# The level products of a gated recurrence as elementwise products summed by a matrix of ones, with level and output work ahead of the weight split and matmul chunks in pairs

## The chip, the cores and the metric

The kernel runs on one core of a Trainium2 chip. The metric is the time of the whole kernel on the device in microseconds (us). The engines of the core that work here are TensorE (PE in the profile, its weight loads PEld), VectorE (DVE), ScalarE (ACT), a little GpSimd (POOL) at the start, and SyncE (SP), whose queue issues the weight loads from HBM.

## What is computed

A trunk of two layers over 256 tokens of width 2048. Layer 0 mixes tokens by a gated linear recurrence (HGRN2), layer 1 by a short gated convolution; each is followed by a gated feed-forward part with 5632 hidden features. Only the recurrence matters here:

```python
D_MODEL = 2048; SEQ = 256; HGRN_HEADS = 16; HGRN_EXPAND = 128; CHUNK = 64

def chunked_gated_recurrence(q, k, v, logf):
    """S_t = diag(f_t) S_{t-1} + k_t v_t^T, o_t = S_t^T q_t, in chunkwise form."""
    ...

def hgrn2_mixer(xn, w_in, lb, out_gain, w_out):
    proj = xn @ w_in
    q, fr, v, g = jnp.split(proj, [HGRN_F_DIM, 2 * HGRN_F_DIM, 2 * HGRN_F_DIM + HGRN_I_DIM], axis=-1)
    q = jax.nn.silu(q.astype(jnp.float32)) * (HGRN_EXPAND ** -0.5)
    f = lb + (1.0 - lb) * jax.nn.sigmoid(fr.astype(jnp.float32))
    k = 1.0 - f
    logf = jnp.log(f)
    o = chunked_gated_recurrence(heads(q), heads(k), heads(v), heads(logf))
    o = rms_norm(o, out_gain) * jax.nn.silu(g.astype(jnp.float32))
    return (o @ w_out.astype(jnp.float32)).astype(xn.dtype)
```

So the output of token t of a head is the sum over s up to t of A[s, t] v_s, where A[s, t] is the dot product, over the head's 128 features, of q_t, k_s and the product of the gates f between s and t.

## The kernel before

**Weights.** Every projection is cut into chunks of 512 input by 256 output features. A chunk is loaded by SP into one of four buffers of `raw`, then split into two parts so that the product keeps float32 accuracy: ACT copies it with rounding to `w_parts[..., 0, :]` (high part, `split` of the scalar block, L325), and DVE subtracts that from the raw value into `w_parts[..., 1, :]` (low part, L542). In the feature-major form PE runs eight 512-column matmuls of the high part (`feature_highs`, L1041) and then eight 256-column matmuls of the low part (`feature_lows`, L1051). In the value group (`V_GROUP`, group 2) the output is token-major: `token_boths` (L1064, both weight parts as the moving operand, counts `lo_used`), then `token_highs` (L1073, counts `hi_used`). ACT may overwrite the buffer of chunk c for chunk c+4 when `hi_used` has counted chunk c; DVE waits for `lo_used` and for ACT's `hi_ready`.

**Phases.** `HGRN_IN` has 4 iterations of 4 groups (gate f, query q, value v, output gate) of 8 chunks each; an iteration serves 4 heads. `HGRN_OUT` has 2 iterations of 2 groups of 8. Then come the two feed-forward parts and the convolution mixer. The steps of a group are in `Phase.steps`; the engines walk the same steps, each with its own program, and meet by semaphores only. PE works a chunk at a time in `HGRN_IN`, `HGRN_OUT` and `DOWN1`, and elsewhere in runs of `RUN` = 2: highs of both chunks, then lows of both.

**Levels.** A is built by nested halves (`LEVELS` = 1, 2, 4 ... 128): the level with half length n pairs a token in the second half of a block of 2n with one in the first. For each level DVE makes `ql` and `kl` (`level_operands`, L769 to L786), PE multiplies them per head as plain float32 128x128 matmuls into the PSUM buffer `side` (L1204), and DVE merges the result into `a_diag` by a mask (`take_stage`, L815). The diagonal is level -1: eight such matmuls of `qh` and `kh` (L1199). DVE carries the prefix products of gates along in `fpre` and `suf` (`prefixes`). `PLAN` says after which chunk of the pair of groups 2 and 3 PE issues which level; numbers above 15 lie in the next iteration. The last stage is the output (`output`, L1183), twelve matmuls of `a_diag`, `a_off` and `vt`.

**Order on DVE and ACT.** At each chunk position DVE first runs the split of the chunk four ahead, then sums a finished accumulator with ACT's copy (`corrected`), then the rest (`pieces`): merge of a level, prefixes, operands. The output is copied from PSUM to `o_sb`, multiplied by gain and gate, split into `act` (`output_steps`, L838 to L849); ACT squares `o_sb`. `act` of iteration 3 is what the last chunks of the first `HGRN_OUT` group wait for.

## Time and profile before

| | |
|---|---|
| time, median of 3 runs | 2345.23 us (2345.22 to 2345.57) |
| the profiled execution | 2345.17 us, span 2343.4 us |
| PE busy | 2330.2 us, 99% |
| DVE busy | 1698.6 us, 72% |
| ACT busy | 1045.2 us, 45% |
| iteration 2 of HGRN_IN (154.04 to 255.94) | 101.90 us, DVE busy 83.64 us |
| HBM | 185 GB/s over the span |

The span is the profiler's, from the first to the last instruction; 1.8 us lie around it. A busy PE is not a PE at its peak, since its matmuls overlap, so the cadence (start to start) tells more than the busy share. The four iterations of HGRN_IN end at about 415 us, HGRN_OUT at about 509 us.

### The profile page before, as it was taken

How to read it: one execution, taken by the hardware profiler on the slowest of the kernel's cores; microseconds unless marked ns; L12 is line 12 of the kernel's file. 1: busy time of each engine (PE TensorE's matmuls, PEld its weight loads, DVE VectorE, ACT ScalarE, POOL GpSimd, SP SyncE). 2: the span in 40 equal slices, each digit the busy share in tenths (PEclk: the TensorE clock that was granted, in tenths of full speed). 3: DMA queues.
4: the chain of work that ended last, by engine and by line, in shares of the span. 5: the costliest groups of instructions: out<-in, count | busy, mean ns of one | idle time of the engine just before them, and what ended most of it. 6: DMA issues, size and time to landing. Idle time of an engine off the chain costs nothing.

```text
span 2343.4 us, 37300 instructions
## 1 busy us (share of the span) xinstructions
PE 2330.2 (99%) x13212; PEld 2048.8 (87%) x13212; DVE 1698.6 (72%) x2151; ACT 1045.2 (45%) x1146; POOL 2.7 (0%) x8
## 2 busy tenths in 40 slices
PE   9999999999999999999999999999999999999998
PEld 8888888888888888888888888888888888888887
DVE  8879788778788788865455766666788788785444
ACT  7344443454444444444444444444444444443443
POOL 0000000000000000000000000000000000000000
PEclk9999999999999999999999999999999999999999
DMA  7555555556656566665656665565656656665564
GB/s 254 159 172 153 166 171 155 179 181 189 188 179 197 186 188 189 188 193 187 194 184 190 186 192 187 186 193 178 198 183 193 192 179 192 190 206 187 191 191 158
DMA packets 410284, 434.93 MB, mean 186 GB/s; under 512 B 13264, under 2 KB 386384, under 8 KB 410064
## 3 DMA queue, kind: packets, MB, share of 16 engines
q1 hardware_dynamic: 409616, 431.53, 59.1%
q10 hardware_dynamic: 576, 2.16, 0.3%
q8 instruction: 59, 0.97, 0.2%
q14 instruction: 33, 0.27, 0.0%
HBM read 431.54 MB, written 2.10 MB: 185 GB/s over the span
## 4 chain that ended last, share of the span: by engine, by line
PE 96%; DVE 2%; DMA 1%; issue 1%; ACT 0%; SPq 0%; DVEq 0%; ACTq 0%
PE acc L1041 54%; PE acc L1051 28%; PE acc L1088 3%; PE acc L1086 3%; PE acc L1087 3%; PE acc L1064 2%; PE side L1204 1%; PE acc L1073 1%; PE side L1183 0%; DMA h<-in_x 0%; DVE w_parts L542 0%; DMA raw<-in_hgrn_w_in 0%; PE side L1199 0%; ACT w_parts L325 0%; DVE kl L778 0%
## 5 line engine op out<-in xcount | busy, mean ns | idle before, releaser
L542 DVE TENSOR_TENSOR w_parts<-raw,w_parts 128x1024 fp32r<-128x1024 f32 x816 | 982.2, 1222 | 575.1 <-PE acc L1051 348.3
L325 ACT ACTIVATE w_parts<-raw 128x1024 fp32r<-128x1024 f32 x816 | 858.1, 1058 | 1023.0 <-PE acc L1041 801.8
L1041 PE MATMUL acc<-xn,w_parts 128*128 128x512 f32 x4352 | 1049.4, 391 | 1.5 <-ACT w_parts L325 1.3
L1041 PEld LDWEIGHTS acc<-xn,w_parts 128*128 128x128 f32 x4352 | 796.5, 188 | 154.0 <-issue 1.5
L1051 PEld LDWEIGHTS acc<-xn,w_parts 128*128 128x128 f32 x4352 | 564.2, 191 | 25.1
L1051 PE MATMUL acc<-xn,w_parts 128*128 128x256 f32 x4352 | 572.4, 283 | 0.0
L1041 PE MATMUL acc<-act,w_parts 128*128 128x512 f32 x1216 | 293.6, 391 | 0.7 <-DVE act L849 0.7
L1041 PEld LDWEIGHTS acc<-act,w_parts 128*128 128x128 f32 x1216 | 222.5, 188 | 43.3 <-DVE act L849 0.9
L1051 PEld LDWEIGHTS acc<-act,w_parts 128*128 128x128 f32 x1216 | 158.0, 191 | 7.2
L1051 PE MATMUL acc<-act,w_parts 128*128 128x256 f32 x1216 | 160.2, 283 | 0.0
L1086 PE MATMUL acc<-w_parts,act 128*128 128x512 f32 x352 | 137.3, 390 | 0.0
L1088 PE MATMUL acc<-w_parts,act 128*128 128x512 f32 x352 | 137.0, 389 | 0.0
L1087 PE MATMUL acc<-w_parts,act 128*128 128x512 f32 x352 | 137.0, 389 | 0.0
L339 ACT ACTIVATE corr<-acc 128x512 f32<-128x512 f32 x144 | 85.7, 595 | 76.0 <-PE acc L1051 76.0
L624 DVE SCALAR_TENSOR_TENSOR tb<-pad,par,tb 128x256 f32<-128x256 f32 x208 | 90.9, 481 | 12.2 <-DVE tb L622 0.3
L624 DVE SCALAR_TENSOR_TENSOR ta<-pad,par,ta 128x256 f32<-128x256 f32 x176 | 77.5, 481 | 11.9
L1088 PEld LDWEIGHTS acc<-w_parts,act 128*128 128x128 f32 x352 | 66.1, 188 | 13.8
L1087 PEld LDWEIGHTS acc<-w_parts,act 128*128 128x128 f32 x352 | 66.1, 188 | 13.6
L1086 PEld LDWEIGHTS acc<-w_parts,act 128*128 128x128 f32 x352 | 66.1, 188 | 13.4
L575 DVE TENSOR_TENSOR pad<-acc,corr 128x512 f32<-128x512 f32 x96 | 65.5, 682 | 0.0
L369 ACT ACTIVATE xn<-h,par 128x256 fp32r<-128x256 f32 x64 | 28.6, 500 | 76.8 <-DVE h L662 59.8
L401 ACT ACTIVATE ta<-ta 128x1024 f32<-128x1024 f32 x22 | 23.4, 1063 | 82.6 <-DVE ta L624 82.6
(125 smaller groups left out, 1024.7 us busy)
## 6 DMA issues: line engine op xcount, KB each, us to landing
raw<-in_ffn_w_up SPq DMA_DIRECT2D x352, 512.0 KB, 3.7
raw<-in_ffn_w_down SPq DMA_DIRECT2D x176, 512.0 KB, 4.5
raw<-in_hgrn_w_in SPq DMA_DIRECT2D x128, 512.0 KB, 3.7
raw<-in_sc_w_in SPq DMA_DIRECT2D x96, 512.0 KB, 4.5
raw<-in_hgrn_w_out SPq DMA_DIRECT2D x32, 512.0 KB, 3.6
raw<-in_sc_w_out SPq DMA_DIRECT2D x32, 512.0 KB, 4.4
h<-in_x SPq DMA_DIRECT2D x4, 512.0 KB, 7.3
final_w<-in_final_norm ACTq DMA_DIRECT2D x1, 1024.0 KB, 7.3
```

The lines of the kernel that those rows point to most:

```text
L325: nc.scalar.activation(w_parts[:, c % RING, :, 0, :], raw[:, c % RING], ACT.Copy).then_inc(hi_ready, 1)
L339: o = nc.scalar.activation(corr[:], acc[:, a % SETS, :, T:], ACT.Copy)
L369: o = nc.scalar.activation(xn[:, bass.ds(tile + j, 1), 0, :], h[:, bass.ds(tile + j, 1), :], ACT.Copy, scale=par[:, bass.ds(weight + tile ...
L542: v.tensor_tensor(w_parts[:, c % RING, :, 1, :], raw[:, c % RING], w_parts[:, c % RING, :, 0, :].bitcast(F32), ALU.subtract).then_inc(lo_r ...
L575: o = v.tensor_tensor(dst[:, part * TW:(part + 1) * TW, :], acc[:, a % SETS, :, 0:T], corr[:], ALU.add)
L624: o = v.scalar_tensor_tensor(out=dst[:, j, :], in0=src, scalar=w, in1=dst[:, j, :], op0=ALU.mult, op1=ALU.add)
L1041: o = mm(to[:, j, :], w[:, q, 0, j * P:(j + 1) * P], src[:, k * KW + q, :, :].rearrange("p n t -> p (n t)"), start=begin and q == 0, stop= ...
L1051: o = mm(to[:, j, T:], w[:, q, 1, j * P:(j + 1) * P], src[:, k * KW + q, 0, :], start=False, stop=end and q == KW - 1, skip_group_check=True)
L1064: o = mm(to[:, b, :], x_block(src, k * KW + q, 0, b), w[:, q].rearrange("p n d -> p (n d)"), start=begin and q == 0, stop=False, skip_grou ...
L1086: mm(bank, x_hi, hi, start=begin and q == 0, stop=False)
L1087: low = mm(bank, x_hi, lo, start=False, stop=False)
L1088: high = mm(bank, x_lo, hi, start=False, stop=end and q == KC - 1)
```

## The change

Four things change.

1. The diagonal and the first level are no longer matmuls of queries with keys. DVE multiplies elementwise (`qh * kh` into `tb`; `ql * kh` into `kl[:, 0]`), ACT rounds the product to its high part (`product_high_parts`), DVE makes the low part (`product_low_parts`), and PE sums over the 128 features by a matrix of ones in float32r matmuls of 512 columns: four for the diagonal, two for the first level. Every row of the result is the same, and the mask picks the place. The parts of the diagonal lie in `act`'s last tiles (`own_parts`).
2. PE works in pairs of chunks in HGRN_IN (but for its very first group) and HGRN_OUT (but for two chunks of its first group). A stage due after an even chunk number then stands between the highs and the lows of a pair.
3. On DVE the level work (merge, prefixes, operands) and the output work stand ahead of the split of the same position, with explicit waits for `stage_done`. `PLAN` puts the diagonal after chunk 3 instead of 2, levels 0 to 3 one chunk later too, and the output after position 17 instead of 18.
4. The output is read straight from PSUM by DVE and ACT (`o_sb` is gone). The first group of HGRN_OUT takes its chunks in another order, in which the part that needs `act` of iteration 3 is at place 6 instead of 5.

```diff
+        elif first and g == 0 and self is HGRN_OUT:
+            order = [(0, 0), (0, 1), (1, 0), (1, 1), (0, 2), (1, 2), (0, 3), (1, 3)]
...
+    def runs(self, first, g, end):
+        single = self is DOWN1 or self is HGRN_IN and first and g == 0
+        paired = 0 if single else self.cpg - RUN if self is HGRN_OUT and first and g == 0 else end
+        return [range(k, k + RUN) for k in range(0, paired, RUN)] + [range(k, k + 1) for k in range(paired, end)]
...
-PLAN = [(2, LEVEL, -1), (3, LEVEL, 0), (5, LEVEL, 1), (6, LEVEL, 2), (8, LEVEL, 3), (10, LEVEL, 4),
-        (12, LEVEL, 5), (13, LEVEL, 6), (15, LEVEL, 7), (18, OUTPUT, 0)]
+PLAN = [(3, LEVEL, -1), (4, LEVEL, 0), (6, LEVEL, 1), (7, LEVEL, 2), (9, LEVEL, 3), (10, LEVEL, 4),
+        (12, LEVEL, 5), (13, LEVEL, 6), (15, LEVEL, 7), (17, OUTPUT, 0)]
...
+            def product_high_parts(i, g, kk):
+                if (g, kk) in ((2, 1), (2, 2)):
+                    act_e.wait_ge(product_ready, at(i, 2, kk))
+                    nc.scalar.activation(own_parts[:, 0] if kk == 1 else pair_parts[:, 0],
+                                         tb[:].rearrange("p j t -> p (j t)") if kk == 1 else
+                                         kl[:, 0].rearrange("p j t -> p (j t)"), ACT.Copy).then_inc(product_hi_ready, 1)
-            phase_of(HGRN_IN, hgrn)
+            phase_of(HGRN_IN, hgrn, ahead=product_high_parts)
...
+                if n == 1:
+                    link(v.tensor_tensor(q_to, halves(qh[:], n)[:, :, 1], pre[:, :, 1], ALU.mult), i)
+                    v.tensor_tensor(kl[:, buf].rearrange("p j (w n) -> p (j w) n", n=n), q_to, halves(kh[:], n)[:, :, 0],
+                                    ALU.mult).then_inc(product_ready, 1)
...
+            def product_low_parts(i, n, product, parts):
+                dve.wait_ge(product_hi_ready, at(i, 2, n + 1))
+                v.tensor_tensor(parts[:, 1], product.rearrange("p j t -> p (j t)"), parts[:, 0].bitcast(F32),
+                                ALU.subtract).then_inc(product_parts_ready, 1)
...
-                    v.tensor_scalar(kl[:, 1], mirrored(fpre[:, :, P:]), -1.0, 1.0, ALU.mult, ALU.add)
...
+                    v.tensor_tensor(tb[:], qh[:], kh[:], ALU.mult).then_inc(product_ready, 1)
+                if n == 1:
+                    product_low_parts(i, 0, tb[:], own_parts)
+                if n == 2:
+                    product_low_parts(i, 1, kl[:, 0], pair_parts)
+
+            def levels(i, first, g, kk):
+                last_take(i, g, kk)
+                if not first:
+                    output_steps(i - 1, g, kk)
+                n = g * HGRN_IN.cpg + kk - 2 * HGRN_IN.cpg
+                done = [stage for stage, (after, what, _) in enumerate(PLAN) if what == LEVEL and n == after + 1]
+                for stage in done:
+                    dve.wait_ge(stage_done, at(i, HGRN_STAGES, S_HGRN + stage + 1))
+                    v.sem_inc(stage_seen, 1)
+                for after, what, m in PLAN:
+                    if what == LEVEL and 0 <= m < len(LEVELS) - 1 and n == operands_at(after, m) + 1:
+                        prefixes(i, m)
                 for after, what, m in PLAN:
-                    if what == LEVEL and m >= 0 and n == after - LEAD:
+                    if what == LEVEL and m >= 0 and n == operands_at(after, m):
                         level_operands(i, m)
+                for stage in done:
+                    take_stage(i, stage)
...
-                        run = 1 if phase in (HGRN_IN, HGRN_OUT, DOWN1) else RUN
-                        for k0 in range(0, phase.cpg - RING * ends_here, run):
+                        for run in phase.runs(first, g, phase.cpg - RING * ends_here):
...
+                        if m < 1:
+                            parts, halves = (own_parts, 2) if m < 0 else (pair_parts, 1)
+                            pe.wait_ge(product_parts_ready, at(i, 2, m + 2))
+                            steps = [lambda to, c=c, n=n: mm(to[:, c * GC:(c + 1) * GC], sum_ones[:],
+                                                             parts[:, n, c * GC:(c + 1) * GC], start=(n == 0),
+                                                             stop=(n == 1))
+                                     for c in range(halves) for n in range(2)]
```

On DVE, at the first two positions of the value group of an iteration of HGRN_IN, before (`w_parts` is a weight split, `qh` the query, `ql` and `kl` the operands of the first level):

```order
L542 TENSOR_TENSOR w_parts<-raw,w_parts 128x4x256 [waits lo_used,hi_ready]
L904 SCALAR_TENSOR_TENSOR qh<-ta,tb 128x1024 [waits gate_sig]
L542 TENSOR_TENSOR w_parts<-raw,w_parts 128x4x256 [waits lo_used,hi_ready]
L769 TENSOR_TENSOR ql<-qh,fpre 128x512 [waits chain]
L776 COPY kl<-kh 128x256 x2
L781 MEMSET suf 128x512
L782 COPY suf<-fpre 128x512
```

and of the change:

```order
L569 TENSOR_TENSOR w_parts<-raw,w_parts 128x4x256 [waits lo_used,hi_ready]
L937 SCALAR_TENSOR_TENSOR qh<-ta,tb 128x1024 [waits gate_sig]
L940 TENSOR_TENSOR tb<-qh,kh 128x1024 [waits qk_ready]
L797 TENSOR_TENSOR ql<-qh,fpre 128x512 [waits chain]
L798 TENSOR_TENSOR kl<-ql,kh 128x512 [waits chain]
L800 MEMSET suf 128x512
L801 COPY suf<-fpre 128x512
L569 TENSOR_TENSOR w_parts<-raw,w_parts 128x4x256 [waits lo_used,hi_ready]
L818 TENSOR_TENSOR act<-tb,act 128x1024 [waits product_hi_ready]
```

The product `tb` and the level's operands now stand ahead of the second split, and the low part of the product (L818) behind it.

On ACT, at the same two positions and the one behind them, of the change (`act` is the high part of the diagonal's product, `pair_parts` that of the first level's; before, the splits stood there with the sigmoid of `tb` alone between the first two):

```order
L340 ACTIVATE w_parts<-raw 128x4x256 [waits hi_used]
L462 ACTIVATE tb<-ta 128x1024 [waits scaled_ready]
L470 ACTIVATE act<-tb 128x1024 [waits product_ready]
L340 ACTIVATE w_parts<-raw 128x4x256 [waits hi_used]
L470 ACTIVATE pair_parts<-kl 128x512 [waits product_ready]
L340 ACTIVATE w_parts<-raw 128x4x256 [waits hi_used]
```

The high part of the product stands ahead of the second split, and waits for DVE's product.

On PE, in the first group of HGRN_OUT from its first chunk that needs `act` of iteration 3 on, before:

```order
L1041 MATMUL acc<-act,w_parts 128x512 [waits hi_ready,act_ready]
L1041 MATMUL acc<-act,w_parts 128x512 x7
L1051 MATMUL acc<-act,w_parts 128x256 [waits lo_ready]
L1051 MATMUL acc<-act,w_parts 128x256 x7
L1041 MATMUL acc<-act,w_parts 128x512 [waits hi_ready]
L1041 MATMUL acc<-act,w_parts 128x512 x7
```

and in the change, from the pair ahead of it:

```order
L1101 MATMUL acc<-act,w_parts 128x512 [waits hi_ready]
L1101 MATMUL acc<-act,w_parts 128x512 x7
L1111 MATMUL acc<-act,w_parts 128x256 [waits lo_ready]
L1111 MATMUL acc<-act,w_parts 128x256 x7
L1111 MATMUL acc<-act,w_parts 128x256 [waits lo_ready]
L1111 MATMUL acc<-act,w_parts 128x256 x7
L1101 MATMUL acc<-act,w_parts 128x512 [waits hi_ready,act_ready]
L1101 MATMUL acc<-act,w_parts 128x512 x7
```

The last wait for `act_ready` has moved from the sixth chunk of the group to the seventh, behind three pairs.

## Rows read from the trace of the kernel before

**Rows 1.** The page: the span, and each engine's busy time, share and instructions.

```profile
span 2343.4 us, 37300 instructions
PE 2330.2 (99%) x13212; PEld 2048.8 (87%) x13212; DVE 1698.6 (72%) x2151; ACT 1045.2 (45%) x1146; POOL 2.7 (0%) x8
```

**Rows 2.** PE's waits: engine, line, releaser, us in total, times, longest us.

```profile
PE side L1204 <- DVE kl L778: 2.3, 4, 0.6
PE acc L1041 <- DVE act L849: 0.7, 1, 0.7
```

**Rows 3.** The chain in a phase of pairs: start us, us, what.

```profile
537.85 3.65 PE acc L1041 x16
...
632.49 3.65 PE acc L1041 x16
```

**Rows 4.** PE's timeline in HGRN_OUT: start, us, engine, line, out<-in, xcount.

```profile
441.95 2.00 PE L1041 MATMUL acc<-act,w_parts 128*128 128x512 f32 x8
...
481.06 1.32 PE L1041 MATMUL acc<-act,w_parts 128*128 128x512 f32 x5
```

**Rows 5.** PE's timeline around the last level of iteration 2.

```profile
210.45 1.06 PE L1204 MATMUL side<-ql,kl 128*128 128x128 f32 x8
211.26 2.09 PE L1041 MATMUL acc<-xn,w_parts 128*128 128x512 f32 x8
213.19 1.11 PE L1051 MATMUL acc<-xn,w_parts 128*128 128x256 f32 x8
214.14 2.00 PE L1041 MATMUL acc<-xn,w_parts 128*128 128x512 f32 x8
215.98 1.12 PE L1051 MATMUL acc<-xn,w_parts 128*128 128x256 f32 x8
```

**Rows 6.** PE's timeline: the diagonal's first matmul, and the first behind it.

```profile
165.21 0.39 PE L1199 MATMUL side<-qh,kh 128*128 128x128 f32 x2
...
166.91 0.47 PE L1064 MATMUL acc<-w_parts,xn 128*128 128x512 f32 x1
```

**Rows 7.** The third level's stage in iteration 2: DVE's operands, then PE.

```profile
179.83 0.75 DVE L778 TENSOR_TENSOR kl<-kh,suf 128x256 f32<-128x256 f32 x2
...
179.86 0.28 PE L1073 MATMUL acc<-w_parts,x_mirror 128*128 128x256 f32 x1
180.71 0.48 PE L1204 MATMUL side<-ql,kl 128*128 128x128 f32 x2 [0.58 <-DVE kl L778]
```

**Rows 8.** PE's timeline: the wait for `act` in HGRN_OUT.

```profile
430.84 1.11 PE L1051 MATMUL acc<-act,w_parts 128*128 128x256 f32 x8
432.61 2.11 PE L1041 MATMUL acc<-act,w_parts 128*128 128x512 f32 x8 [0.65 <-DVE act L849]
```

**Rows 9.** The value group's start in iteration 2: PE, ACT and DVE.

```profile
156.83 0.40 PE L1064 MATMUL acc<-w_parts,xn 128*128 128x512 f32 x1
...
159.82 1.06 ACT L325 ACTIVATE w_parts<-raw 128x1024 fp32r<-128x1024 f32 x1 [2.11 <-PE acc L1073]
160.79 1.04 ACT L443 ACTIVATE tb<-ta 128x1024 f32<-128x1024 f32 x1
...
160.92 1.23 DVE L542 TENSOR_TENSOR w_parts<-raw,w_parts 128x1024 fp32r<-128x1024 f32 x1 [0.66 <-ACT w_parts L325]
162.06 1.22 DVE L904 SCALAR_TENSOR_TENSOR qh<-ta,tb 128x1024 f32<-128x1024 f32 x1
```

**Rows 10.** DVE's timeline: split of position 3, and the last level's key operand.

```profile
171.09 1.23 DVE L542 TENSOR_TENSOR w_parts<-raw,w_parts 128x1024 fp32r<-128x1024 f32 x1 [2.60 <-ACT w_parts L325]
...
208.13 0.67 DVE L771 TENSOR_TENSOR kl<-kh,suf 128x512 f32<-128x512 f32 x1
```

**Rows 11.** PE's opening matmuls (L1169) in two stretches: busy us (count), clock, DMA.

```profile
1.00:4.60 3.60, 3.52 (x16) 3.55 (x17) 1.00 0.73 226
4.60:6.60 2.00, 2.00 (x18) 1.86 (x16) 1.00 1.06 400
```

More of the change, by code:

```diff
@@ L212, in trunk @@
         stage_free = sem("stage_free")
+        stage_seen = sem("stage_seen")
         inits = sem("inits")
@@ L340, in correction, with phase_of @@
                 o.then_inc(corr_ready, 1)
-            def phase_of(phase, pieces, peel_last=False):
+            def phase_of(phase, pieces, peel_last=False, ahead=None):
                 def body(i, first):
@@ L420, in output_steps @@
                 if (g, kk) == (0, 3):
[L421 to L422 removed]
+                    s = S_HGRN + HGRN_STAGES - 1
+                    act_e.wait_ge(act_ready, at(i, 1, 1))
+                    nc.scalar.activation(qh[:], side[:, s % STAGES].rearrange("p (j t) -> p j t", j=TG), ACT.Square) \
+                        .then_inc(sq_ready, 1)
             def hgrn(i, first, g, kk):
@@ L519, in body @@
                             if ahead:
-                                ahead(i, g, kk)
+                                ahead(i, first, g, kk)
                             early = first and phase is HGRN_IN and g == 0
@@ L634, in normed, with residual_phase @@
                 add_squares(i, 4, sq + part, sq + part, ta[:, part * TW:(part + 1) * TW, :])
-            def residual_phase(phase, r0, sq0, weight, rs_n=None, rs_stage=None):
+            def residual_phase(phase, r0, sq0, weight, rs_n=None, rs_stage=None, ahead=None):
                 carry = carried.pop() if carried else None
@@ L665, in pieces @@
                         normed(i, phase, r, sq, part, tile, weight)
-                phase_of(phase, pieces, into=lambda g: tb)
+                phase_of(phase, pieces, ahead=ahead, into=lambda g: tb)
             def up_phase(phase, n, rs_n, rs_stage, conv):
@@ L877, in hgrn @@
                     rms(0, S_RS_HGRN, T + 2)
-                for stage, (after, _, _) in enumerate(PLAN):
-                    if n == after + 1:
-                        take_stage(i, stage)
                 if kk == last and g != V_GROUP:
@@ L894, in hgrn @@
                     v.tensor_scalar(kh[:], fpre[:], -1.0, 1.0, ALU.mult, ALU.add)
-                    v.tensor_scalar(kl[:, 1], mirrored(fpre[:, :, P:]), -1.0, 1.0, ALU.mult, ALU.add)
-                for after, what, m in PLAN:
-                    if what == LEVEL and 0 <= m < len(LEVELS) - 1 and n == after - LEAD + 1:
-                        prefixes(i, m)
                 if not first:
-                    output_steps(i - 1, g, kk)
+                    output_sums(i - 1, g, kk)
                 if n == 0:
@@ L905, in hgrn, with last_output @@
                                            op0=ALU.mult, op1=ALU.mult).then_inc(qk_ready, 1)
-                    dve.wait_ge(qk_ready, at(i, 1 + len(LEVELS), 1))
+                    dve.wait_ge(qk_ready, at(i, len(LEVELS), 1))
+                    v.tensor_tensor(tb[:], qh[:], kh[:], ALU.mult).then_inc(product_ready, 1)
[11 more added lines that the diff above has]
+                    dve.wait_ge(stage_done, at(i, HGRN_STAGES, S_HGRN + stage + 1))
+                    v.sem_inc(stage_seen, 1)
                 for after, what, m in PLAN:
-                    if what == LEVEL and m >= 0 and n == after - LEAD:
+                    if what == LEVEL and 0 <= m < len(LEVELS) - 1 and n == operands_at(after, m) + 1:
+                        prefixes(i, m)
+                for after, what, m in PLAN:
+                    if what == LEVEL and m >= 0 and n == operands_at(after, m):
                         level_operands(i, m)
-            phase_of(HGRN_IN, hgrn, ahead=last_take, into=lambda g: ta)
+                for stage in done:
+                    take_stage(i, stage)
+            phase_of(HGRN_IN, hgrn, ahead=levels, into=lambda g: ta)
             late[0] += 4 * HGRN_IN.n
-            carried.append(lambda g, kk: output_steps(HGRN_IN.n - 1, g, kk))
-            residual_phase(HGRN_OUT, 0, 8, NORM_FFN, 1, S_RS_OUT)
+            carried.append(lambda g, kk: output_sums(HGRN_IN.n - 1, g, kk))
+            def last_output(i, first, g, kk):
+                if first:
+                    output_steps(HGRN_IN.n - 1, g, kk)
+            residual_phase(HGRN_OUT, 0, 8, NORM_FFN, 1, S_RS_OUT, ahead=last_output)
             up_phase(UP0, 0, 2, S_RS_UP0, FFN_CONV)
@@ L1149, in body @@
                             if phase is DOWN1:
-                                between(i, first, g, k0)
+                                between(i, first, g, run[0])
                                 continue
-                            for kk in range(k0, k0 + run - 1):
+                            for kk in run[:-1]:
                                 between(i, first, g, kk)
@@ L1159, in body @@
                                     feature_lows(to, c, src, k, end)
-                            between(i, first, g, k0 + run - 1)
+                            between(i, first, g, run[-1])
                         if ends_here:
```

95 lines of the change are left out of this document (47 added, 48 removed).

## The prediction

> **What bounds the kernel now.** The page's busy shares come first: PE is busy 99% of the span, DVE 72%, ACT 45% [rows 1]. So the time is PE's, and an edit is worth what it takes from PE's own stream or from its waits. PE's waits come next, and they are few: four on a level's operands, 2.3 us, and one on the activations of HGRN_OUT, 0.7 us [rows 2]. The rest is cadence. I therefore read PE's timeline by starts, and then the timelines of DVE and ACT where the change puts new work between them and PE. An iteration of HGRN_IN takes 101.9 us; whatever is found in it counts four times.
>
> **The change part by part.**
>
> *Pairs.* In the phase of pairs 17 pairs lie between the two starts shown, 94.64 / 17 = 5.567 us each [rows 3]. Chunk by chunk 14 chunks take 39.11 us, 2.794 each, 5.587 per two [rows 4]. A pair saves 0.020 us. HGRN_IN gets 60 pairs (4 iterations of 16, less 4 in its first group), HGRN_OUT 15: 75 x 0.020 = **-1.5 us**. That a stage falls inside a pair changes the count of switches between highs and lows by none.
>
> *A level's stage now.* Four float32 matmuls take 0.81 us to the next start, and the eight matmuls behind them need 1.93 where an undisturbed eight need 1.84: 0.90 us in all [rows 5]. The diagonal has eight of them: 166.91 - 165.21 = 1.70, plus the same 0.09, 1.79 us [rows 6].
>
> *The stages as sums by ones.* The trace has no matmul with a matrix of ones in this format, but it has 512-column matmuls of the same format by the thousand: 3.65 / 16 = 0.228 us [rows 3]. Four are 0.91 us, two 0.46. They can't be quicker, since they stream the same columns; if they paid the 0.09 us of a change of operand [rows 5], they would be 1.00 and 0.55. I take the lower, because they are of the format of their neighbours. Diagonal 1.79 - 0.91 = 0.88, first level 0.90 - 0.46 = 0.44; 1.32 x 4 = **-5.3 us** (-4.6 at the other end).
>
> *Waits that go.* Before the third level PE pauses: 180.71 - 179.86 = 0.85 where 0.12 is the cadence, 0.73 us, and some 0.1 us of restart behind it, as the stage behind a pause is that much longer in the timeline. The change gives that level one more chunk. 0.84 x 4 = **-3.4 us** [rows 2, 7]. In HGRN_OUT PE starts at 432.61 where 430.84 + 0.95 = 431.79 was due, a wait of 0.82 [rows 8]. Now the output comes one chunk earlier and the chunk that needs it one later, and DVE does its product ahead of the split: 5.6 us more room. **-0.8 us**. What is late next there is the root of the norm; its start moves by 0.6 us (one accumulator is summed ahead of it), and PE asks for the next splits more than a microsecond after they are ready.
>
> Without anything new, these make -11.0 us. Now what is new.
>
> *The wait that comes: the product's way to PE.* The diagonal's product goes DVE, ACT, DVE, and weight splits stand in between on both. I time it from the start of the value group (156.83 in iteration 2 [rows 9]), with the durations of rows 9: an ACT pass over 1024 elements 1.06, 0.97 to the next start; a DVE pass 1.22 or 1.23, 1.14 to the next start; 0.04 from ACT's end to DVE's start (160.88 to 160.92), which I take for DVE's own result and for DVE to ACT too.
>
> - ACT may split chunk 4 when `hi_used` has counted chunk 0. Now this is at 2.79, and ACT starts at 2.99 [rows 9]. In pairs the eight highs of chunk 1 come in front: 3.65 + 0.95 = 4.61, ACT at 4.81.
> - DVE's split 1.10 later, as in rows 9: 5.91. The query at 7.05, done 8.27. The product at 8.31, done 9.53.
> - ACT's next instruction is the product's high part, 9.57. Only then its split of chunk 5, 10.55 to 11.61.
> - DVE has meanwhile made the first level's operands (0.67 us and less each [rows 10]; done about 11.5). It waits for that split: 11.65. Its low part of the product starts at 12.79, done 14.01.
> - PE gets it 0.13 us later, as with the level before (180.58 to 180.71 [rows 7]): **14.14**.
>
> PE gets there after two pairs: 2 x 5.567 = **11.13**. So it waits 3.0 us, plus the 0.1 of restart: 3.1 us, in each iteration, **+12.4 us**. Queued behind it is all of PE's work. Who waits in turn is nobody in need: chunk 4 and 5 are split by 7.1 and 12.9, and due at 15.1 and 16.9. The uncertainty is the hand-over times, eight of them, and whether the splits between are of the usual length: 2.6 to 3.6 us, 10.4 to 14.4 in all.
>
> *DVE behind that wait.* DVE gains three passes over the products and a product more (about 3.5 us) and loses the copy of the output and the small key copies (about 2.3). In the trace it works from the split of position 3 (171.09) to the last level's key operand (208.80) with hardly a pause, 37.7 us [rows 10]. In the change that split starts at 12.79 + 1.14 + 1.14 + two passes over 512 elements (0.67 or less) = 16.3 to 16.4; one split fewer (1.14) lies on the way, as levels now stand ahead of it: ready at 16.4 + 37.7 - 1.1 = 53.0. PE comes to the last level at 14.14 + 0.1 + 0.91 + 12 chunks (33.4) + 0.46 + six levels (5.4) = 54.4. So DVE arrives 1.4 us early, and for the level before, by the same count, about 1. The wait at the diagonal pays for this: without it PE would be there at 51.3, and DVE late by 1.8. DVE's six new marks (`stage_seen`) have no row of their own; between nothing and the 0.13 us hand-over of rows 7 each, 0 to 0.8 us. I take it that they fit.
>
> *Others at nothing.* The ones' memset is behind POOL's own first ones. Reading the output in PSUM costs DVE as much as reading the copy; ACT's square starts after the product. The output one position earlier: `a_off` is merged ahead of the split at the iteration's end and PE needs it two chunks later. SP's loads wait for the low splits; the latest of these is the one at 12.9, and its load is needed nine us later.
>
> **Sum.** -1.5 - 5.3 - 3.4 - 0.8 + 12.4 = +1.4 us. The profiled execution took 2345.17 us against a median of 2345.23, so they can stand for each other: **2346.6 us**. The gain in PE's stream is real and a new wait eats it. A measurement of this kernel can tell about 0.2%, 4.7 us, from no change.
>
> **The rivals.**
>
> *The wait does not come, or is short.* If ACT or DVE were through by 11.13, all of the first part would count, less what DVE owes at the last level: -11.0 + 4 x 1.8 = -3.8 at the worst, -11.0 at best, **2334 to 2341**, 2337 in the middle. For it: in the trace the query is made as late as 162.06 only because ACT's split is, and a smaller hand-over or another order in the queues would move all. Against it: the seven steps are all in program order with a semaphore each, and three microseconds are two and a half DVE passes. 11%.
>
> *TensorE's clock falls in the pause* (the slower side). The opening matmuls show both levels: 16 records in 3.6 us, then 18 in 2.0 [rows 11], so 1.2 GHz and then 2.4 GHz, though the clock column reads 1.00 in both. PE's pauses in the trace are all much shorter than 3 us, and none is followed by slow matmuls. If this one were, the work behind it would run at half rate as long as the opening did, 3.6 us, and lose 1.8 us: 2346.6 + 4 x 1.8 = **2353.8**. It decides from the pause that is long enough for the clock to fall, which no row shows; the stream before and behind is dense. 7%.
>
> The Trainium skill ("TensorE: Matmul & The Clock Gate", the section on HAM oscillation) says that a kernel whose matmul bursts are parted by pauses can be throttled again at each pause and start every burst cold. That is this rival; the trace has no pause to test it on.
>
> *DVE becomes the bound behind the wait.* Once the marks and waits cost DVE over 1 us more than counted by position 11 to 13, PE waits at the last two levels. Each further microsecond is 4 us in all; at 1.0 over, **2350.6**. For it: DVE has no pause in that stretch. Against: the count keeps one merge in reserve. 14%.
>
> *The stages save nothing* (operand changes cost what the columns save): +5.3, 2351.9; it needs the sums by ones to be twice as slow as every row of their kind. 2%.
>
> **How the numbers follow.** The forecast has 66%, with its own range 2344 to 2349.5 from the wait's 10.4 to 14.4 us and the stage's 0.7. The range of eight in ten takes in the upper part of the first rival and the DVE case: 2340 to 2351. Faster by over 0.2% (under 2340.5): 11% of the first rival, less its slow end, and a little of the forecast: 0.12. Slower by over 0.2% (over 2349.9): the clock, half of the DVE case, the stages and the forecast's edge: 0.16. Within: 0.72.
>
> **What would show it.** PE's waits after: a releaser DVE, the subtraction into `act`, four times about 3 us, and no wait on `kl` nor on HGRN_OUT's activations. The stage of the diagonal 0.9 us, that of the first level 0.46. An iteration of 102.4 us instead of 101.9. DVE without a pause from the second split of the value group to the last level. If the matmuls behind the pause have a cadence of 0.43 us, the clock fell. I am wrong if ACT's high part of the product starts well before 9.6 us from the group's start, or if the last levels show waits.

## The result and the profile after

| | before | changed |
|---|---|---|
| median of 11 executions | 2345.23 us | 2351.47 us |
| lowest and highest | 2344.91, 2345.60 | 2346.86, 2354.06 |
| profiled execution, its span | 2345.17, 2343.4 | 2348.86, 2347.0 |
| ratio, 95% interval | | 1.0023 (1.0015 to 1.0031) |

The change makes the kernel 0.15 to 0.31% slower. The forecast was 2346.6 us, the range 2340 to 2351. The median of all executions lies 0.5 us above the range; the ratio times 2345.23 gives 2350.6, just inside. The kernel before had 0.7 us between its lowest and highest execution. Now it is 7.2 us, and that spread is the first thing to explain: the lowest execution is the forecast to 0.3 us.

The page of the changed kernel, first the span and busy times, as in [rows 1]:

```profile
span 2347.0 us, 37183 instructions
...
PE 2325.6 (99%) x13140; PEld 2044.5 (87%) x13140; DVE 1703.4 (73%) x2151; ACT 1050.2 (45%) x1154; POOL 2.8 (0%) x9
```

PE has 4.6 us less to do and a span 3.6 us longer. Its waits, answering to [rows 2]:

```profile
PE side L1259 <- DVE act L818: 11.1, 4, 2.8
PE acc L1101 <- ACT w_parts L340: 1.4, 2, 1.2
```

Both old waits are gone, the one on `kl` and the one on the activations of HGRN_OUT. In their place stands one in front of the diagonal's sums, four times. Both waits of the second row lie in the program's first 30 us. PE's timeline of the value group in iteration 2 (start, us, what; "..." leaves out matmuls of the chunks):

```profile
159.65 0.40 PE L1124 MATMUL acc<-w_parts,xn 128*128 128x512 f32 x1
...
170.67 0.28 PE L1133 MATMUL acc<-w_parts,x_mirror 128*128 128x256 f32 x1
173.74 1.19 PE L1259 MATMUL side<-act,sum_ones 128*128 128x512 f32 x4 [2.79 <-DVE act L818]
174.76 0.39 PE L1124 MATMUL acc<-w_parts,xn 128*128 128x512 f32 x1
...
178.41 0.62 PE L1259 MATMUL side<-pair_parts,sum_ones 128*128 128x512 f32 x2
178.87 0.28 PE L1133 MATMUL acc<-w_parts,xn 128*128 128x256 f32 x1
...
276.28 1.19 PE L1259 MATMUL side<-act,sum_ones 128*128 128x512 f32 x4 [2.79 <-DVE act L818]
```

Two pairs end where the third should start, 170.67 + 0.12 = 170.79, which is 11.14 us after the group's start. PE goes on at 173.74, or 14.09. The first level's two sums take 178.87 - 178.41 = 0.46 us, the diagonal's four 1.02 behind the pause, 0.91 and the restart. From this diagonal to that of the next iteration it is 276.28 - 173.74 = 102.54 us, where an iteration took 101.9. The steps that make PE wait, from the timelines of ACT and DVE:

```profile
164.46 1.06 ACT L340 ACTIVATE w_parts<-raw 128x1024 fp32r<-128x1024 f32 x1 [3.93 <-PE acc L1133]
...
169.20 1.06 ACT L470 ACTIVATE act<-tb 128x1024 fp32r<-128x1024 f32 x1 [2.74 <-DVE tb L940]
170.17 1.04 ACT L340 ACTIVATE w_parts<-raw 128x1024 fp32r<-128x1024 f32 x1
...
165.55 1.22 DVE L569 TENSOR_TENSOR w_parts<-raw,w_parts 128x1024 fp32r<-128x1024 f32 x1 [2.37 <-ACT w_parts L340]
166.69 1.22 DVE L937 SCALAR_TENSOR_TENSOR qh<-ta,tb 128x1024 f32<-128x1024 f32 x1
167.95 1.23 DVE L940 TENSOR_TENSOR tb<-qh,kh 128x1024 f32<-128x1024 f32 x1
...
171.24 1.23 DVE L569 TENSOR_TENSOR w_parts<-raw,w_parts 128x1024 fp32r<-128x1024 f32 x1
172.39 1.22 DVE L818 TENSOR_TENSOR act<-tb,act 128x1024 fp32r<-128x1024 f32 x1
```

The steps form one chain through both queues: ACT's split stands ahead of DVE's split, DVE's split ahead of the query (166.69) and the product (167.95), then ACT's high part (169.20), ACT's next split (170.17), DVE's of the same chunk (171.24), and only then the low part, done at 173.61.

From 170.67 to 173.74 are 3.07 us from start to start. Less the cadence of 0.12 that is a wait of 2.95 us, four times 11.8, or 12.2 with the 0.1 us of restart behind each. Two places where something is saved follow. First HGRN_OUT, where the eight highs at 439.40 are the first that need `act` of iteration 3. They start 16 x 0.12 us after the sixteen lows before them, without the wait of [rows 8]:

```profile
433.83 3.82 PE L1101 MATMUL acc<-act,w_parts 128*128 128x512 f32 x16
437.49 2.08 PE L1111 MATMUL acc<-act,w_parts 128*128 128x256 f32 x16
439.40 2.00 PE L1101 MATMUL acc<-act,w_parts 128*128 128x512 f32 x8
```

Second, the pairs: the chain in a phase that is in pairs in both kernels keeps its rate, as in [rows 3], three pairs in 16.70 us, 5.567 each:

```profile
535.94 3.65 PE acc L1101 x16
...
552.64 3.65 PE acc L1101 x16
```

The profiled execution is still 2.0 us above the lowest one. The cause is in the matmuls behind one of the four pauses, the one of the first iteration:

```profile
69.45 1.46 PE L1259 MATMUL side<-act,sum_ones 128*128 128x512 f32 x4 [2.77 <-DVE act L818]
70.71 0.63 PE L1124 MATMUL acc<-w_parts,xn 128*128 128x512 f32 x1
71.14 0.63 PE L1124 MATMUL acc<-w_parts,x_mirror 128*128 128x512 f32 x1
```

They start 0.43 us apart where those of iteration 2 start 0.23 apart. The view by stretches of 4.55 us from the diagonal's first sum shows the granted clock (the number before the last two; ahead of it the busy times of PE, PE's weight loads, DVE, ACT and POOL, behind it the DMA share and GB/s), here for the first and second iteration:

```profile
69.45:74.00 4.55, 4.55 (x13) 3.60 (x14) 4.55 (x7) 0.69 (x2) 0.00 (x0) 0.62 0.72 208
173.74:178.29 4.55, 4.55 (x20) 3.77 (x21) 4.55 (x7) 0.61 (x2) 0.00 (x0) 1.00 0.73 205
```

13 matmuls instead of 20 in the same time, at a mean clock of 0.62 instead of 1.00: for most of that stretch PE ran at 1.2 GHz instead of 2.4. Eight gaps of 0.427 us instead of 0.228 are **1.6 us for one fall**, of the 2.0 us. The same comes out from the diagonal's first sum to the first level's first: 6.30 us in this iteration and 4.68 in the next. The Trainium skill ("TensorE: Matmul & The Clock Gate", the section on HAM oscillation) says that a kernel with pauses between its bursts of matmuls can be throttled again in each pause. Behind this pause the trace shows just that; behind the other three, which are as long, it shows no fall.

### The profile page after: what moved, and what is told of

It reads as the page before. It is cut to its first block, busy times and chain, and to the rows that moved or that the text cites. A ratio compares the mean times of both kernels' runs of the same rounds, so it can differ in the third digit from the quotient of the medians.

```text
span 2347.0 us, 37183 instructions
## 1 busy us (share of the span) xinstructions
PE 2325.6 (99%) x13140; PEld 2044.5 (87%) x13140; DVE 1703.4 (73%) x2151; ACT 1050.2 (45%) x1154; POOL 2.8 (0%) x9
## 4 chain that ended last, share of the span: by engine, by line
PE 97%; DVE 1%; issue 1%; DMA 1%; ACT 0%; DVEq 0%; ACTq 0%; SPq 0%
PE acc L1101 54%; PE acc L1111 28%; PE acc L1146 3%; PE acc L1147 3%; PE acc L1148 3%; PE acc L1124 2%; PE side L1265 1%; PE acc L1133 1%; PE side L1242 0%; DMA raw<-in_hgrn_w_in 0%; DVE w_parts L569 0%; PE side L1259 0%; ACT w_parts L340 0%; DVE act L818 0%; DVE qh L937 0%
## 5 line engine op out<-in xcount | busy, mean ns | idle before, releaser
L1111 PE MATMUL acc<-xn,w_parts 128*128 128x256 f32 x4352 | 566.4, 283 | 0.0
L651 DVE SCALAR_TENSOR_TENSOR tb<-pad,par,tb 128x256 f32<-128x256 f32 x208 | 90.9, 481 | 12.2 <-DVE tb L649 0.3
```

The lines of the kernel that those rows point to most:

```text
L651: o = v.scalar_tensor_tensor(out=dst[:, j, :], in0=src, scalar=w, in1=dst[:, j, :], op0=ALU.mult, op1=ALU.add)
L1111: o = mm(to[:, j, T:], w[:, q, 1, j * P:(j + 1) * P], src[:, k * KW + q, 0, :], start=False, stop=end and q == KW - 1, skip_group_check=True)
```

## The experiments

Two questions: does the pause with its clock falls make up the whole loss, and what would the kernel take without the pause? Beside these runs the kernel before took 2345.1 to 2345.3 us. Where the text takes a time without a fall of the clock, it is that of the change's lowest execution, 2346.86 us.

**The pause filled.** Ten sums of ones over other data, whose results are overwritten, ahead of PE's wait.

```diff
+                            if m < 0:
+                                pe.wait_ge(stage_free, at(i, HGRN_STAGES, S_HGRN + s + 1))
+                                for _ in range(10):
+                                    mm(side[:, (S_HGRN + s) % STAGES, 0:GC], sum_ones[:],
+                                       xn[:, 0].rearrange("p n t -> p (n t)"), start=True, stop=True)
                             pe.wait_ge(product_parts_ready, at(i, 2, m + 2))
```

> The changed kernel with ten extra 512-column matmuls (10 x 0.228 = 2.3 us) on TensorE just ahead of its wait for the diagonal's product parts, into the PSUM region that the stage overwrites. Nothing else differs. The pause of 3.0 us keeps its end (set by VectorE), but TensorE idles only about 0.7 us of it. Theory (a clock fall behind some of the four pauses makes the spread of 2346.9 to 2354.1 us): every run at 2346.5 to 2347.3, no matmul of 0.43 us cadence, spread under 0.5 us. Rival (the spread comes from elsewhere, DMA or VectorE): the same spread and a median near 2351.

Measured: 2346.7 us (2346.25 to 2347.24, 11 executions), ratio 1.0006 (0.9997 to 1.0015). The wait is now

```profile
PE side L1264 <- DVE act L818: 1.7, 4, 0.5
```

and no matmul of HGRN_IN has the slow cadence. The work and the wait for the product are those of the change, and the time is 4.8 us less, with a spread of 1.0 us, where under 0.5 was expected. So the falls of the clock made the rest: the median with the pause filled is the change's lowest execution to 0.2 us.

**The pause longer.** DVE makes the diagonal's low part twice.

```diff
                 dve.wait_ge(product_hi_ready, at(i, 2, n + 1))
+                if n == 0:
+                    link(v.tensor_tensor(parts[:, 1], product.rearrange("p j t -> p (j t)"), parts[:, 0].bitcast(F32),
+                                         ALU.subtract), i)
```

> The changed kernel with VectorE's low part of the diagonal's product computed twice, so that each of the four pauses of TensorE is 1.2 us longer, 4.1 to 4.2 us. Theory (clock falls by the length of the pause): it falls in most or all of the four, 2346.9 + 4.8 + 4 x 1.4 to 1.8 = 2357.5 to 2359, and the spread gets narrower. Rival (a fall depends on something else than the pause): 2346.9 + 4.8 = 2351.7 at the low end with the spread of before, median near 2356.

Measured: 2358.84 us (2358.35 to 2359.60, 5 executions). PE's wait, and the stretch behind the pause of the second iteration:

```profile
PE side L1262 <- DVE act L821: 16.2, 4, 4.1
```

```profile
175.82:180.37 4.55, 4.55 (x13) 3.59 (x14) 4.55 (x7) 0.00 (x0) 0.00 (x0) 0.62 0.49 153
```

All four pauses, now 4.3 us from start to start, have it. The sum closes: 2346.9 + 4 x 1.26 of longer pause + 4 x 1.6 = 2358.3, 0.5 us under the median; the profiled execution took 2358.35. With every pause followed by a fall the spread is small again.

**The value group chunk by chunk, all else as in the change.**

```diff
-        single = self is DOWN1 or self is HGRN_IN and first and g == 0
+        single = self is DOWN1 or self is HGRN_IN and (first and g == 0 or g == V_GROUP)
```

> The changed kernel with the value group of HGRN_IN done chunk by chunk, all else in pairs. Theory: hi_used counts its first chunk 1.8 us earlier, so the parts of the product are there 12.3 us after the group's start instead of 14.1, and TensorE's pause is 1.1 to 1.2 us instead of 3.0; no clock fall. 2346.9 - 4 x 1.8 + 16 pairs x 0.02 = 2340, spread under 0.5 us. Rival (VectorE is the bound behind the pause): the last levels' operands come late by what the pause lost, 2344 or more.

Measured: 2339.64 us (2339.28 to 2339.99, 10 executions), ratio 0.9976 (0.9966 to 0.9985). The wait and the stretch behind it in iteration 2:

```profile
PE side L1259 <- DVE act L818: 3.8, 4, 0.9
```

```profile
168.09:172.64 4.55, 4.55 (x24) 3.91 (x25) 4.55 (x7) 1.41 (x4) 0.00 (x0) 1.00 0.69 199
```

The median is 11.8 us under the change's: 4.6 are the falls of the clock (2351.47 - 2346.86), 7.2 the pause. In pairs the eight 512-column matmuls of the second chunk (`token_boths`, 8 x 0.228 us) stand ahead of the 256-column ones of the first (`token_highs`, which count `hi_used`), so ACT gets to its first split, and every step behind it to its place, 1.8 us later. The 16 pairs in this group save 16 x 0.020 = 0.3 us and cost 4 x 1.85 (3.07 - 1.22) = 7.4, and the clock.

**No pair in HGRN_IN and HGRN_OUT.**

```diff
-        single = self is DOWN1 or self is HGRN_IN and first and g == 0
+        single = self in (DOWN1, HGRN_IN, HGRN_OUT)
```

> The changed kernel with TensorE chunk by chunk in all of HGRN_IN and HGRN_OUT. Theory: as e3 (2339.6), less the gain of 59 more pairs at 0.020 us: 2340.8; the pause at the diagonal 0.9 to 1.2 us, no clock fall. Rival (stages after an even chunk now come 0.9 us earlier and meet VectorE late): some waits of level stages more, 2342 to 2344.

Measured: 2340.84 us (2340.51 to 2341.11, 11 executions), 1.2 us above the kernel with the value group alone unpaired. For 59 pairs fewer that is 0.020 us each, the rate read from [rows 3, 4].

**No wait for the diagonal's product.** PE sums data that are there already.

```diff
-                            pe.wait_ge(product_parts_ready, at(i, 2, m + 2))
+                            if m == 0:
+                                pe.wait_ge(product_parts_ready, at(i, 2, m + 2))
                             steps = [lambda to, c=c, n=n: mm(to[:, c * GC:(c + 1) * GC], sum_ones[:],
-                                                             parts[:, n, c * GC:(c + 1) * GC], start=(n == 0),
+                                                             (parts[:, n, c * GC:(c + 1) * GC] if halves == 1 else
+                                                              xn[:, 2 * c + n].rearrange("p n t -> p (n t)")),
+                                                             start=(n == 0),
```

> The changed kernel in which TensorE's sums of the diagonal read columns of the normed input instead of the product's parts, so that it doesn't wait for them; VectorE and ScalarE still make the parts, and the diagonal of the attention is wrong. Theory (VectorE owes about 1.8 us at the last level once the pause is gone): no pause at the diagonal, waits of 1 to 2 us in each iteration at the level sums behind it, 2337 to 2341. Rival (VectorE has room): 2334.5 to 2336, no waits on kl.

Measured: 2346.11 us (2345.70 to 2346.45, 10 executions). The range was missed by 5 us: a wait of 11.8 us is gone, and against 2346.86 only 0.8 us is saved. PE's waits, then DVE and PE around the third level in iteration 2:

```profile
PE side L1268 <- DVE a_diag L842: 5.8, 8, 1.2
PE side L1260 <- DVE pair_parts L818: 2.3, 4, 0.6
```

```profile
182.02 0.69 DVE L813 TENSOR_TENSOR suf<-suf,fpre 128x512 f32<-128x512 f32 x1
182.63 1.29 DVE L842 COPY_PREDICATED a_diag<-masks,side 128x512 f32<-128x512 uint8 x1
...
182.68 0.28 PE L1133 MATMUL acc<-w_parts,x_mirror 128*128 128x256 f32 x1
183.98 1.16 PE L1268 MATMUL side<-ql,kl 128*128 128x128 f32 x8 [1.02 <-DVE a_diag L842]
```

The third level's operands are long there (`suf`, behind them, begins at 182.02). PE waits for its output buffer: `side` has two, and this stage may start when DVE has merged the stage two before it out of PSUM (182.63 to 183.92), which stands in DVE's queue behind prefixes and operands. In the changed kernel that merge ends (184.98 + 1.31 = 186.29) 0.95 us before PE starts its stage, at 187.24. By starts, less the cadence, the waits for a buffer in iteration 2 are 1.17 us at this level and 0.55 at a later one, and the one for the first level's product (the second row) is 0.73. With some 0.1 us of restart behind each, four iterations lose about 11 us again. So the pause at the diagonal was also what kept DVE in time.

**Query, product and low part ahead of the split.**

```diff
                 n = g * HGRN_IN.cpg + kk - 2 * HGRN_IN.cpg
+                if n == 0:
+                    dve.wait_ge(gate_sig, at(i, 3, 2))
+                    v.scalar_tensor_tensor(out=qh[:], in0=ta[:], scalar=float(P) ** -0.5, in1=tb[:],
+                                           op0=ALU.mult, op1=ALU.mult).then_inc(qk_ready, 1)
+                    dve.wait_ge(qk_ready, at(i, len(LEVELS), 1))
+                    v.tensor_tensor(tb[:], qh[:], kh[:], ALU.mult).then_inc(product_ready, 1)
...
+                if n == 0:
+                    product_low_parts(i, 0, tb[:], own_parts)
+                if n == 2:
+                    product_low_parts(i, 1, kl[:, 0], pair_parts)
```

and these lines go from their old place behind the split; `operands_at` gives 0 for the first level, and ACT's sigmoid moves ahead of its split likewise.

> The changed kernel with the query's sigmoid on ScalarE and, on VectorE, the query, the diagonal's product, the first level's operands and the low part of the diagonal's product all ahead of the split of the value group's first position, and the low part of the first level's product ahead of the third split. Pairs stay. Theory (VectorE's whole chain from the query to the last level is late because its first link is queued behind a split that waits for a pair): the query starts about 4.7 us after the group's start instead of 7.0, the diagonal's parts are ready at 10.5 to 10.7, before TensorE comes at 11.13; no pause there, no clock fall, and the level waits of run e4 (2.5 us an iteration) shrink to 0 to 0.3 us. 2334.2 to 2336, spread under 0.5 us. Rival (VectorE's busy time bounds the stretch, wherever the query starts): waits on the level stages as in e4, 2342 or more.

Measured: 2340.92 us (2340.69 to 2341.38, 11 executions), ratio 0.9981. PE passes the diagonal without a pause, and this is left:

```profile
PE side L1267 <- DVE a_diag L845: 4.1, 8, 0.7
```

```profile
180.40 0.28 PE L1135 MATMUL acc<-w_parts,x_mirror 128*128 128x256 f32 x1
181.29 1.16 PE L1267 MATMUL side<-ql,kl 128*128 128x128 f32 x8 [0.61 <-DVE a_diag L845]
```

This is the same hand-back of the buffer as in the kernel above, less late since DVE has begun earlier. The steps came as expected: the query starts 4.66 us after the group's start, and the diagonal's parts are ready at 10.42. The time is again 5 us over the range, for the same reason.

**The same with the old float32 matmuls** for the diagonal and first level:

```diff
-                            steps = [lambda to, c=c, n=n: mm(to[:, c * GC:(c + 1) * GC], sum_ones[:],
-                                                             parts[:, n, c * GC:(c + 1) * GC], start=(n == 0),
-                                                             stop=(n == 1))
-                                     for c in range(halves) for n in range(2)]
+                            steps = [lambda to, j=j, b=b: mm(to[:, (halves * j + b) * P:(halves * j + b + 1) * P],
+                                                             kh[:, j, 0:P], qh[:, j, b * P:(b + 1) * P],
+                                                             start=True, stop=True)
+                                     for j in range(TG) for b in range(halves)]
```

> Run e5 with the diagonal and the first level done on TensorE by the float32 128x128 matmuls of before (eight and four, of kh and qh), at the same places and with the same waits; the products are still made but not used, and both results are wrong. Theory (the stages' price is as in the sum): 1.32 us more in each iteration, e5 + 5.3. Rival (later arrival of TensorE relieves VectorE, or the sums by ones pay changes of operand): e5 + 3.5 to 4.6.

Measured: 2341.03 us (2340.93 to 2341.66, 11 executions), the same as with sums by ones. Both expectations missed. Where DVE's hand-back sets PE's time, what is taken from PE's stream comes back as wait. With the old matmuls, 1.3 us longer in an iteration, PE's gap ahead of the third level, from start to start, falls from 0.89 to 0.12 us, the one ahead of a later level from 0.68 to 0.37: 1.1 us less wait, and less restart behind it.

**The merge first.** The kernel with the query ahead, and DVE merges a stage as soon as it is done, before prefixes and operands.

```diff
                 for stage in done:
                     dve.wait_ge(stage_done, at(i, HGRN_STAGES, S_HGRN + stage + 1))
                     v.sem_inc(stage_seen, 1)
+                    take_stage(i, stage)
...
-                for stage in done:
-                    take_stage(i, stage)
```

> Run e5 with the merge of a finished level (which gives the PSUM buffer back) ahead of the prefixes and operands at the same position, not behind them. Theory (the waits left in e5, 4.1 us on the merge and some 1.2 us of restarts, are for the buffer, while the next operands are ready a microsecond earlier): those waits go, the operands are still in time by 0 to 0.5 us, 2334.5 to 2337. Rival (VectorE's total work up to the last levels is the bound, in whatever order): waits on kl take the place of those on a_diag, 2339 to 2341.

Measured: 2338.22 us (2338.05 to 2338.63, 7 executions), ratio 0.9970 (0.9958 to 0.9981): the fastest here, 7.0 us under the kernel before. The wait on `a_diag` is gone; PE's wait, then the operands and PE in iteration 2:

```profile
PE side L1266 <- DVE kl L812: 1.7, 4, 0.4
```

```profile
200.01 0.75 DVE L812 TENSOR_TENSOR kl<-kh,suf 128x256 f32<-128x256 f32 x2
...
200.89 1.15 PE L1266 MATMUL side<-ql,kl 128*128 128x128 f32 x8 [0.42 <-DVE kl L812]
```

Now a level's operands are late, as in [rows 7], only in another place, as the rival said. The time lies between the two ranges (2334.5 to 2337 and 2339 to 2341), so both missed: the waits for the buffer are gone, and 0.58 us of wait for the operands are left in each iteration by starts, with the restart behind it and two waits under 0.15.

**The same with the old matmuls.**

> Run e9 with the diagonal and the first level done by the float32 128x128 matmuls of before, as in e6 (their results are wrong). Theory: where TensorE waits for nobody, the stages' saving counts in full, e9 + 5.3 us; where VectorE is still the bound in e9, e9 + 1 to 4.

Measured: 2339.68 us (2339.36 to 2340.03, 10 executions), no wait of a level in the trace, inside the second range of the expectation. The sums by ones are worth 1.5 us here, of the 5.3 that they take out of PE's stream; the rest is waited for.

**How long may the pause be?** Four filling matmuls instead of ten leave pauses of 2.2 us from start to start.

```diff
-                                for _ in range(10):
+                                for _ in range(4):
```

> Run e1 with four extra matmuls instead of ten ahead of the wait, so that TensorE idles 2.0 to 2.1 us at each of the four places while the wait's end stays. Theory (a fall needs a pause of nearly the 3.0 us at which some fell): no falls, 2346.5 to 2347.3, spread under 0.7 us. Rival (shorter pauses fall too, more seldom): spread up to 2 us or more.

Measured: 2348.08 us. Two of eleven executions took 2346.80 and 2346.87, the other nine 2347.98 to 2348.65. A miss: no fall was expected. The profiled one was of the two and has no slow matmul, so the kernel was run once more for a profile:

> The kernel of run e8 once more, for a profile of an execution at 2348.1 rather than 2346.8, as nine of its eleven runs were. Theory (the clock falls behind one of the four 2.1 us pauses): some six to eight matmuls with 0.43 us from start to start behind one of them. Rival: no such matmuls, the 1.3 us lie elsewhere.

Measured: 2348.38 us. The stretches behind the first pause (2.24 us) and the second (2.18):

```profile
69.20:73.75 4.55, 4.55 (x13) 3.64 (x14) 4.55 (x7) 0.68 (x2) 0.00 (x0) 0.63 0.74 211
173.38:177.93 4.55, 4.55 (x20) 3.74 (x21) 4.55 (x7) 0.69 (x2) 0.00 (x0) 1.00 0.65 195
```

There is one fall, and behind it 6.26 us from the diagonal's first sum to the first level's, where the next iteration has 4.71. That the nine slower executions each had one fall is inferred from their times; behind which pause, their times don't tell.

**The changed kernel once more**, for a second profiled execution:

> The changed kernel once more, unedited, for a second profiled execution. Its executions lay between 2346.9 and 2354.1 us; the first profiled one, 2348.86 us, has matmuls at 0.43 us behind one of its four pauses at the diagonal. Theory (the clock alone makes the spread): the time is 2346.9 us plus 1.3 to 1.8 us for each of the four pauses that has such slow matmuls behind it in the trace, so two of them go with 2349.5 to 2350.5, four with 2352.1 to 2354.1; the waits recorded at the diagonal stay 2.7 to 2.8 us each. Rival (something else makes the spread, as longer waits or slower transfers): a time that this count misses by over 1 us, with the difference in PE's waits or spread over the program.

Measured: 2348.51 us. The waits at the diagonal are 2.8 us each again. The first and the fourth iteration:

```profile
69.09:73.64 4.55, 4.55 (x20) 3.78 (x21) 4.55 (x7) 0.69 (x2) 0.00 (x0) 1.00 0.67 210
376.82:381.37 4.55, 4.55 (x14) 3.62 (x15) 4.55 (x7) 0.60 (x2) 0.00 (x0) 0.66 0.68 204
```

```profile
376.82 1.19 PE L1259 MATMUL side<-act,sum_ones 128*128 128x512 f32 x4 [2.80 <-DVE act L818]
377.85 0.39 PE L1124 MATMUL acc<-w_parts,xn 128*128 128x512 f32 x1
378.08 0.44 PE L1124 MATMUL acc<-w_parts,x_mirror 128*128 128x512 f32 x1
378.31 0.63 PE L1124 MATMUL acc<-w_parts,xn 128*128 128x512 f32 x1
378.74 0.63 PE L1124 MATMUL acc<-w_parts,x_mirror 128*128 128x512 f32 x1
```

This is again one fall and the time of one fall (2346.9 + 1.6 = 2348.5), but behind the fourth pause, while the first is without. So it isn't the place in the program; pauses of the same length, with the same work around them, are followed by a fall or not. Neither profiled execution shows two or more falls. That the six slower executions of the change (2351.47 to 2354.06) are those with three or four is inferred: from their distance to the lowest, 4.6 to 7.2 us at 1.6 a fall; from their mean clock, 0.996 and 0.997 against 0.998 and 0.999, where the trace with four falls (low part twice) has 0.997; and from the filled pause, which takes the spread away. Four falls make 2353.3, so the last 0.8 us of the slowest execution are not explained.

## Why the prediction came out as it did

*The mechanism and its sum were right.* Term by term:

| term | predicted | in the trace of the change |
|---|---|---|
| a pair | 5.567 us | 5.567; unpairing costs 0.020 a pair |
| diagonal, first level | 0.91, 0.46 | 1.02 with the restart, 0.46 |
| waits on `kl` and in HGRN_OUT | gone | gone |
| PE at the diagonal, after the group's start | 11.13 | 11.14 |
| its operands ready | 14.14 | 14.09 |
| last level's key operand ready, PE there | 53.0, 54.4 | 52.4, 54.4 |
| iteration 2 | 102.4 us | 102.54 |
| all, without a fall of the clock | 2346.6 us | 2346.86 |

The eight hand-overs of the ladder were out by 0.05 us in all. The lengths of the passes came from rows of the same engine and size. Only the 0.04 us from one result to the next step was carried over from one pair of engines to the others; it measured 0.04 from DVE to DVE and 0.02 from DVE to ACT. The prediction's "eight highs of chunk 1" are, in the value group, the eight matmuls of `token_boths`; they have the same 512 columns, so the sum is not touched.

*The step that failed is the chance of the clock rival, 7%.* Its mechanism (a fall in the pause, 0.43 us cadence behind it) and its price (1.8 us a fall; measured 1.6) stood in the text. But I gave it as four falls or none, and as unlikely because every pause in the trace of before is much shorter: a row that doesn't exist speaks for neither side. By their times, ten of eleven executions had at least one fall; the trace of the profiled one shows it. The rival's 2353.8 is near the upper end of what happened, 2354.06; the forecast, 2346.6, is the lower end, and the median is between. The range's upper end came out of the DVE case at 2350.6, and cut the clock's off. A range that held all the falls would have reached 2354. That the ratio's 2350.6 still lies inside is luck: the upper end stood for a DVE wait that did not come.

*The forecast case "within 0.2%"* had 0.72. The interval, 0.15 to 0.31% slower, lies across the bound. It isn't settled for either side, and it leans to "slower", which had 0.16, and the median of all executions, 0.27% slower, lies beyond it.

*The rival of no wait left a dependency out.* I put the kernel without a pause at 2334 to 2341, 2337 in the middle, from DVE's lateness at the last level (1.8 us). With the steps earlier it took 2340.9, with PE's wait alone taken away 2346.1, and with the merge first too 2338.2. The count had the way of DVE's operands to PE, but not the way back: the merge that frees one of two `side` buffers, due already at the third level. So what the pause costs and what ends its cost are two things: PE gains only as far as DVE's queue comes forward too.

*DVE as the bound behind the wait* (14%) did not come: the last level's key operand is ready (211.37 + 0.68 = 212.05) 2.0 us before PE starts, where 1.4 was worked out; these are from DVE's and PE's timelines in iteration 2:

```profile
211.37 0.68 DVE L805 TENSOR_TENSOR kl<-kh,suf 128x512 f32<-128x512 f32 x1
...
214.05 1.06 PE L1265 MATMUL side<-ql,kl 128*128 128x128 f32 x8
```

*That the stages save nothing* (2%) is refuted as it was meant, in PE's cadence. In what the kernel gains it is nearly true wherever DVE sets the pace: 0.1 and 1.5 us of 5.3.

## To carry to other kernels

Before an edit shortens the busiest engine's stream, follow each buffer back to it too: with two output buffers the consumer's place in its own queue is a deadline like any operand. An order that is better for one engine (pairs) can put the head of a chain through three engines later; keep it out of the one group where such a chain starts (2339.6 us here), or put the chain's head ahead of the splits and free a buffer before preparing the next operands (2338.2 us, with the pairs kept). The two together were not run. Where a forecast puts a new pause into TensorE's stream that is longer than any in the trace, count a clock fall behind each as an open cost, from none to all, and let the range hold both ends.

## What the runs showed of the hardware

TensorE's clock fell from 2.4 to 1.2 GHz at some of the new pauses, and not at each. From the start of the last matmul before the pause to the start of the first behind it:

| pause | kernel | falls |
|---|---|---|
| under 0.9 us | pause filled with ten | none of 4 |
| 1.2 us | value group chunk by chunk; no pairs at all | none of 4 in each |
| 1.3 to 1.5 us | no wait for the product (third level) | none of 4 |
| 2.2 us | pause filled with four | none of 4 and 1 of 4 (two profiled executions) |
| 3.1 us | the change | 1 of 4 and 1 of 4 (two profiled executions) |
| 4.3 us | low part twice | 4 of 4 |

A fall costs 1.5 to 1.6 us in the traces, from the diagonal's first sum to the first level's. The slow matmuls need not be the first ones behind the pause: in the last experiment the four sums and the first two matmuls behind them (376.82 to 378.31) have the full rate, and the cadence of 0.43 us begins with the third. What decides which pause of a kind is hit, no run here shows.
